# First layer's modulation columns: weight pieces stationary and two condition columns moving, in place of condition columns stationary and weight rows moving

## What is computed

```python
silu_c = jax.nn.silu(c)
silu_cc = jax.nn.silu(c_ctx)
mod = (silu_c @ ada_w[l] + ada_b[l])[:, None, :]
sh1, sc1, g1, sh2, sc2, g2 = jnp.split(mod, 6, axis=-1)
hx = modulate(rms_norm(x, norm_mix_w[l]), sh1, sc1)
cmod = (silu_cc @ ada_w[l] + ada_b[l])[None, None, :]
csh1, csc1, cg1, csh2, csc2, cg2 = jnp.split(cmod, 6, axis=-1)
hc = modulate(rms_norm(cx, norm_mix_w[l]), csh1, csc1)
```

## Time and profile before

| what | value |
|---|---|
| median of 3 runs | 1295.59 us (1290.89 to 1298.23) |
| profiled execution, own time | 1300.01 us |
| its span | 1298.1 us |
| mean granted TensorE clock | 0.911 |
| PE busy / PEld / DVE / ACT / POOL | 84% / 58% / 69% / 44% / 13% of the span |
| HBM read | 308 MB, 255 GB/s over the span with what is written |

### The profile page before, as it was taken

The page is one execution under the profiler, slowest core; times in us unless marked ns, Lnnn a source line. Parts: engine busy times, 40 slices in busy tenths (PEclk is TensorE's granted clock), DMA queues, the critical chain, the costliest instruction groups (busy, mean ns, idle before and its releaser), DMA issues. The chain is left out here.

```text
span 1298.1 us, 13257 instructions
## 1 busy us (share of the span) xinstructions
PE 1093.1 (84%) x4594; PEld 758.7 (58%) x4594; DVE 894.7 (69%) x1005; ACT 568.4 (44%) x578; POOL 171.0 (13%) x170
## 2 busy tenths in 40 slices
PE   6699999997799994399999999709629999999980
PEld 1344443445466443278888888608417888888870
DVE  0476775843567124679999999552576999999964
ACT  1411111111256103267777777311236777777741
POOL 0100210000100000401111110040032111111005
PEclk9799999999689997599999999958759999999995
DMA  8656684633200014479999999375347999999936
GB/s 338 245 203 244 227 332 171 239 135 125 86 1 1 1 65 137 135 277 410 413 414 413 412 414 413 127 280 198 137 124 247 410 414 414 414 414 413 412 150 226
DMA packets 141977, 332.00 MB, mean 256 GB/s; under 512 B 10480, under 2 KB 12472, under 8 KB 141808
## 3 DMA queue, kind: packets, MB, share of 16 engines
q1 hardware_dynamic: 127768, 288.60, 58.8%
q0 software_dynamic: 7488, 25.19, 5.0%
q10 hardware_dynamic: 6680, 17.67, 3.4%
HBM read 308.32 MB, written 23.15 MB: 255 GB/s over the span
## 5 line engine op out<-in xcount | busy, mean ns | idle before, releaser
L1468 DVE TENSOR_TENSOR w_lo<-ring,w_hi 128x2048 fp32r<-128x2048 f32 x192 | 428.3, 2285 | 27.7 <-ACT w_hi L1307 27.7
L1307 ACT CAST w_hi<-ring 128x2048 fp32r<-128x2048 f32 x192 | 362.6, 1910 | 74.5 <-PE bank L1585 49.0
L1585 PE MATMUL bank<-w_hi,xT_hi 128*128 128x512 f32 x512 | 205.5, 401 | 10.5 <-DVE xT_lo L1473 10.5
L1585 PE MATMUL bank<-w_hi,xT_lo 128*128 128x512 f32 x512 | 201.8, 394 | 0.0
L1585 PE MATMUL bank<-w_lo,xT_hi 128*128 128x512 f32 x512 | 201.6, 394 | 0.0
L1585 PEld LDWEIGHTS bank<-w_hi,xT_hi 128*128 128x128 f32 x512 | 97.8, 191 | 31.4 <-DVE xT_lo L1473 12.1
L958 PE MATMUL bank<-ring_last,arena 128*128 128x512 f32 x256 | 113.1, 597 | 0.0
L698 DVE SCALAR_TENSOR_TENSOR gate_b<-ring,silu_c,gate_b 128x512 f32<-128x512 f32 x140 | 107.4, 767 | 5.0
L958 PE MATMUL bank<-ring,arena 128*128 128x512 f32 (+1 forms) x256 | 109.4, 582 | 1.6 <-ACT arena L476 1.6
L1585 PEld LDWEIGHTS bank<-w_hi,xT_lo 128*128 128x128 f32 x512 | 97.5, 190 | 21.0
L1585 PEld LDWEIGHTS bank<-w_lo,xT_hi 128*128 128x128 f32 x512 | 97.8, 191 | 19.3
(11 more groups left out here) (224 smaller groups left out, 1243.5 us busy)
## 6 DMA issues: line engine op xcount, KB each, us to landing
ring<-in_moe_w_gate SPq DMA_DIRECT2D x64, 1024.0 KB, 9.3
ring<-in_moe_w_up SPq DMA_DIRECT2D x64, 1024.0 KB, 11.4
ring<-in_moe_w_down SPq DMA_DIRECT2D x64, 1024.0 KB, 9.5
ring<-in_ada_w SPq DMA_DIRECT2D x23, 2048.0 KB, 7.8
y_scratch<-arena ACTq DMA_DIRECT2D x32, 512.0 KB, 6.0
ring<-in_w_in SPq DMA_DIRECT2D x3, 2048.0 KB, 9.6
ring_last<-in_w_in SPq DMA_DIRECT2D x3, 2048.0 KB, 8.8
xh_scratch<-arena SPq DMA_DIRECT2D x8, 512.0 KB, 2.6
```

What stands on the lines that cost most here:

```text
L1307: nc.scalar.copy(w_hi[:, buf(u, p), :], half(raw(e, p))).then_inc(s_hi, 3 if isinstance(e, int) and (e, p) == (-1, 3) else 1)
L1468: V.tensor_tensor(w_lo[:, buf(u, p), :], half(raw(e, p)), w_hi[:, buf(u, p), :].bitcast(F32), ALU.subtract).then_inc(s_lo, 3 if isinstance ...
L1585: last = pe.matmul(bank[:, b, :], xs[:, kk, :], ws[:, k, :], start=(kk == 0 and i == 0), stop=(kk == KD - 1 and i == 2))
```

## The change

The products of the four slabs are turned round. For each slab and each of its four blocks of 128 columns, and each of the 8 pieces `k`, the 128x128 weight piece becomes stationary and the two condition columns move. The result is already a 128x2 column pair, and all 16 pairs lie side by side in bank 4, where the transposes put them before. The copies to `pre_rows`, the 16 transposes and the semaphores `m_prc` and `m_prt` go. The number of products rises from 4 x 8 = 32 to 4 x 4 x 8 = 128.

```diff
@@ semaphores
-        m_pre = sem("m_adaln_rows_of_slab")
-        m_prc = sem("m_adaln_rows_copied")
-        m_prt = sem("m_adaln_rows_transposed")
+        m_pre = sem("m_adaln_columns_of_slab")
@@ memory
-        pre_rows = arena[0:2, at_rope:at_rope + 2 * D]
@@ VectorE
                 dve.wait_ge(m_cols, 2)
-                for j in range(PRE):
-                    dve.wait_ge(m_pre, j + 1)
-                    nc.vector.tensor_copy(pre_rows[:, j * HALF:(j + 1) * HALF], bank[0:2, 4 + j, :]).then_inc(m_prc, 1)
-                dve.wait_ge(m_prt, 1)
+                dve.wait_ge(m_pre, PRE)
@@ TensorE
                 for j in range(PRE):
                     w = slab_in(j, 1)
-                    for k in range(KD):
-                        last = pe.matmul(bank[0:2, 4 + j, :], silu_c[:, :, k], w[:, k, :], start=(k == 0), stop=(k == KD - 1))
+                    for q in range(HALF // P):
+                        col = 2 * (j * (HALF // P) + q)
+                        for k in range(KD):
+                            last = pe.matmul(bank[:, 4, col:col + 2], w[:, k, q * P:(q + 1) * P], silu_c[:, :, k],
+                                             start=(k == 0), stop=(k == KD - 1))
                     last.then_inc(m_pre, 1)
-                pe.wait_ge(m_prc, PRE)
-                for j in range(2 * KD):
-                    last = pe.transpose(bank[:, 4, 2 * j:2 * j + 2], pre_rows[:, j * P:(j + 1) * P], ident[0:2, 0:2])
-                last.then_inc(m_prt, 1)
```

## The result

The changed kernel takes 1322.9 us (median of 4 runs, 1315.2 to 1323.8), the kernel before, beside it, 1296.9 us. The ratio is 1.0191, 95% interval 1.0135 to 1.0247: slower, clear of no change; whether by more or by less than 2% is not settled. A second series gave 1321.9 against 1299.0 us, ratio 1.0180, 1.0144 to 1.0216. The forecast was 1321.5. The profiled execution has a span of 1321.9 us, 23.8 more than before.

A forecast was written before the change was run, and what follows sets the result against it. TensorE and then the six-tile chain bound the start; the projection has no slack. At the lower clock: +25.3 to the first tile, +0.9 for tile 2, so +26.2 on 1295.6 gives 1321.8, rounded to 1321.5; range 1302 to 1328.

The forecast's parts named there:

- I take the lower level, for all four slabs: New products before the projection: TensorE's clock stays at 1.2 GHz, pairs cost 0.218 us; chance 0.78.
- almost nothing moves: Reason for expecting 1.2 GHz: the new products load 128 columns and move only 2.
- Rival 1: New products: the clock rises at 16.1 as before, -0.6 to -1.8 us, about 1294.5; chance 0.12.
- no rise recorded before the projection: Sign in the profile after: PEclk 0.5 or no clock rise recorded before the projection would show the forecast.
- 0.218: New products: spacing in us per pair of weight load and matmul at 1.2 GHz, putting the products' end at 68.1.
- lower bound of 0.21: New products: pair spacing in us bounded from below by the lengths of loads; it would give -2.0 us.
- removed chain: Behind the last product: last copy, 16 transposes and handovers go, from 41.73 to 43.68, 1.95 us.
- Tile 2's transposes had run at 1.09 and will take 1.97: +0.9: Tiles before the projection: tile 2's transposes run at the lower clock level, delaying the projection by 0.9 us.
- each waiting for the one before: From 43.57 to 61.52: six tiles form one chain, so a delay of the first moves everything behind it.
- Hidden loads: SyncE's second `w_in` slab goes out at 68 and lands at 77, ten microseconds before the projection, costing nothing.
- The block: From the projection to the end everything shifts as a block, by +26.2 us.
- Either way by 2 us: In the projection: the instant of the clock's rise can shift either way by 2 us.

The follow-up runs named there:

- third experiment: Changed kernel with six idle products of 512 moving columns before the first slab lands, to bring the clock up first; one run, 1317.8 us.
- first experiment: Changed kernel with 128 columns moved in place of 2, the two conditions repeated 64 times; 1296.0 us, ratio 0.9994 to the kernel before.
- second profile: The changed kernel run once more, unchanged, for a narrower interval; 1321.9 us, ratio 1.0180 to the kernel before.
- last-slab kernel: Kernel before the change with only the last slab in the new form, slabs 0 to 2 in the old; one run, 1297.2 us.

## Why the prediction was right, point by point

**The clock.** The step that carried everything was "I take the lower level, for all four slabs", called a judgment. It held: spacing 0.213 for all 256 pairs. No row of the kernel before could decide it, so this is a judgment that came out, and not a reading; the reason given, that almost nothing moves, is at least too narrow, since 64 columns did no better. The third experiment shows the fall under these very products, and the first shows the same weight pieces at the higher level. Why the chip grants it to the one and not to the other no run shows. Rival 1 fails although TensorE and its loads were busy 54.78 of 54.78 us. Its page, "TensorE: Matmul & The Clock Gate" of the Trainium skill, section "Why this matters for your kernels", asks to keep TensorE busy continuously; by this trace that was not enough. One of the signs named, no rise recorded before the projection, failed in this profile (a rise at 70.0, behind the products) and held in the second one (89.5).

**The pair price.** 0.218 was taken, from five intervals of the earlier trace rows; it measured 0.213. The lower bound of 0.21 was the better guide. Over 255 pairs the difference is 1.2 us: products ended at 67.0 where 68.1 was said. The same page of the Trainium skill gives 107 ns for a load of 128 columns, in its section "LDWEIGHTS (loading the stationary operand)". The pairs at the higher level agree with it (0.107 us in the third experiment, 0.112 in the first), and those of the changed kernel take twice as long.

**The removed chain.** 1.95 us was right but for a handover that stays: 0.12 us lie now between last product and bias add, and 1.8 were gained in the first experiment.

**The tiles.** "Tile 2's transposes had run at 1.09 and will take 1.97: +0.9" is the one term that failed. They took 1.76, which is +0.7, and nothing of it reached the projection: from the first tile's read to the projection there are 16.83 us, and 16.81 before. Tile 3's transposes start 6.7 us behind the first read in both kernels, tile 5's 13.3 us; tile 4's alone are 0.7 later. The tiles run as two strands, even and odd, since a tile's square sum stands behind the read of the tile two before it. A delay of tile 2 goes to tile 4, and the last tile, 5, is odd. The second profile is the cleaner test: tile 2's transposes took the forecast 1.97 there, tile 4's came 0.9 later than before, and from the first tile's read (68.88) to the projection (85.69) there are still 16.81 us. That the prediction called the tiles a chain, "each waiting for the one before", was its error here. Without this term and with 0.213 the sum is +24.1, which is what the projection shows.

**Hidden loads.** The second `w_in` slab went out at 67.03 and at the 7.9 us which the DMA list of the page gives for its line it landed near 75, over ten ahead of need; the projection's wait names ScalarE alone.

**The block.** +24.15 at the projection, +23.8 at the end: it held in this pair of profiles, but not stage by stage. The difference is +23.4 at the start of the attention stage (359.27 for 335.84), +25.0 at its end (437.04 for 412.00) and +23.8 at the end of all, so deviations of over 1 us cancelled. The last-slab kernel shows that the block need not hold, by 10 us, of which 6.8 go with when the higher level came in two stretches. "Either way by 2 us" fits the rise in the projection, where the eleven profiles differ by 2.0 us in all (272.3 to 274.3); it left out the attention stage, which can add 5 to 6. Over medians this did little harm. That the forecast's 1321.5 lies so near to 1322.9 is partly luck: it had 2 us too much at the projection, and the medians moved by 26.0 us in the first series and by 22.9 in the second.

## What to carry to other kernels

Turning a product round so that the large operand is stationary trades moving columns for loaded ones, nearly one for one: for one slab, 16 pairs that move 512 took 7.03 us and 64 pairs that load 128 took 7.31 at the higher level. Price it at both levels of the clock (the changed kernel's last slab took 13.79), and look at what the engine then moves: in these runs series of 128-column loads stayed at the lower level with 2 and with 64 moving columns, although TensorE was busy without a gap, and reached the higher one with 128. Where a stationary operand is only a few columns wide, put blocks on different column groups first; and when a stall goes, look at what the next engine's own queue still has to issue.

## What was not expected of the hardware

- More moving columns were faster: 128 in place of 2, for the same result, took 23 us off a stage of 55 us.
- 64-column loads of float32 on different column halves ran beside each other at 0.0535 us a pair, on the same half at 0.107. The Trainium skill, in "TensorE: Matmul & The Clock Gate", section "The mechanism", says that loads overlap with matmuls in flight only where the row groups differ. These pairs all used the same 128 rows, and their overlap hung on the column half; the measurement decides.
- The level came up for a moment in the changed kernel, from 70.0 to 73.4, and since 67.0 TensorE had done nothing but 16 transposes. In the second profile of the same kernel it did not: TensorE did the same work, and the first rise is at 89.5. So one profile of such a moment says little.
- The attention stage, same code, took 71 us or 76 to 78, with the higher level granted 14 us into it or 28 and more.
